# Transformer block pair with a 64-expert layer: shared expert's weights and a fourth set of expert places in dead arena rows

## The reference, cut to what matters

```python
def moe_ffn(h, w_router, b_router, w_e_gate, w_e_up, w_e_down, w_sh_gate, w_sh_up, w_sh_down):
    scores = jax.nn.sigmoid(h @ w_router)
    _, idx = lax.top_k(scores + b_router, TOP_K)            # 8 of 64 experts for each token
    ...
    yb = swiglu(h_pad[tok], w_e_gate[e], w_e_up[e], w_e_down[e]) * wt[:, None]
    ...
    return swiglu(h, w_sh_gate, w_sh_up, w_sh_down) + routed[:n]
```

## Time and profile before

| | |
|---|---|
| median of 3 runs | 1839.1 us (1836.88 to 1841.07) |
| the profiled execution's own time | 1846.18 us |
| its span (first to last instruction) | 1844.1 us |
| mean granted TensorE clock | 0.970 |
| PE, DVE, ACT, POOL busy | 91%, 45%, 30%, 2% |
| read from HBM | 416.07 MB, 227 GB/s over the span |
| SyncE's queue, share of 16 DMA engines | 58.8% |
| expert loop, first `pair_hidden` to the last one's start | 471.47 to 997.69 us |

### The profile page before, as it was taken

How to read it: one execution, slowest core, us unless ns; L and a number is a source line. 1 busy time by engine, 2 the same in 40 slices (tenths; PEclk the granted TensorE clock), 3 DMA queues, 4 the chain that set the end, 5 groups by cost and what they waited for, 6 DMA issues and landing times.

```text
span 1844.1 us, 22609 instructions
## 1 busy us (share of the span) xinstructions
PE 1675.3 (91%) x8972; PEld 1165.0 (63%) x8973; DVE 825.2 (45%) x1187; ACT 561.9 (30%) x795; POOL 41.4 (2%) x49
## 2 busy tenths in 40 slices
PE   2699999998899999899999799989999799989998
PEld 2674554546444444444444677779998677779997
DVE  1811982314322222222221676585444575675544
ACT  0001442002111111111111456644432456644441
POOL 2200000000000000000000000000000000000000
PEclk9999999998999999999999899989999899989999
DMA  9552488232899999899998443545554443535640
GB/s 261 180 209 97 168 306 309 102 98 89 327 374 392 375 395 387 350 388 387 382 381 339 145 165 121 200 137 182 169 176 163 148 147 137 190 130 183 206 160 23
DMA packets 148297, 418.62 MB, mean 227 GB/s; under 512 B 6960, under 2 KB 55104, under 8 KB 123168
## 3 DMA queue, kind: packets, MB, share of 16 engines
q1 hardware_dynamic: 143472, 399.12, 58.8%
q0 software_dynamic: 4720, 18.03, 3.2%
HBM read 416.07 MB, written 2.95 MB: 227 GB/s over the span
## 4 chain that ended last, share of the span: by engine, by line
PE 84%; DVE 7%; issue 5%; DMA 2%; ACT 1%; SPq 0%; DVEq 0%; ACTq 0%
PE bank L1414 14%; PE bank L1140 13%; PE bank L1241 12%; PE bank L847 9%; PE bank L1151 6%; PE bank L1394 6%; PE bank L1122 4%; PE bank L1161 3%; PE bank L816 3%; PE bank L1254 3%; PE bank L974 3%; DMA weight_ring<-in_w_ada 2%; PE bank L860 2%; DVE arena L1746 1%; DVE ring_low L2198 1%
## 5 line engine op out<-in xcount | busy, mean ns | idle before, releaser
L1140 PE MATMUL bank<-weight_ring,arena 128*64 128x512 f32 x1056 | 239.7, 607 | 40.2 <-issue 39.3
L2198 DVE TENSOR_TENSOR ring_low<-weight_ring,high_ring 128x2048 fp32r<-128x2048 f32 x94 | 211.5, 2288 | 62.2 <-ACT high_ring L1557 55.1
L1241 PE MATMUL bank<-high_ring,split 128*128 128x512 f32 x640 | 212.5, 406 | 0.0
L1140 PEld LDWEIGHTS bank<-weight_ring,arena 128*64 128x64 f32 x1056 | 87.5, 139 | 191.1 <-issue 191.1
L1414 PE MATMUL bank<-split,high_ring 128*128 128x256 f32 x1088 | 198.6, 286 | 3.1 <-issue 3.1
L1414 PE MATMUL bank<-split,ring_low 128*128 128x256 f32 x704 | 200.6, 285 | 0.0
L1557 ACT ACTIVATE high_ring<-weight_ring 128x2048 fp32r<-128x2048 f32 x94 | 175.2, 1903 | 17.7 <-PE bank L1241 8.5
L1414 PEld LDWEIGHTS bank<-split,high_ring 128*128 128x128 f32 x1088 | 170.9, 193 | 4.6 <-issue 3.9
L847 PE MATMUL bank<-weight_ring,arena 128*128 128x512 f32 (+1 forms) x416 | 163.2, 552 | 2.1 <-ACT arena L1447 1.3
L1241 PE MATMUL bank<-ring_low,split 128*128 128x512 f32 x384 | 154.0, 401 | 0.0
L1241 PEld LDWEIGHTS bank<-high_ring,split 128*128 128x128 f32 x640 | 124.0, 194 | 32.4 <-issue 3.4
(11 more groups left out here) (284 smaller groups left out, 2244.6 us busy)
## 6 DMA issues: line engine op xcount, KB each, us to landing
weight_ring<-in_w_e_gate SPq DMA_DIRECT2D x65, 1024.0 KB, 7.6
weight_ring<-in_w_e_up SPq DMA_DIRECT2D x65, 1024.0 KB, 9.7
weight_ring<-in_w_e_down SPq DMA_DIRECT2D x65, 1024.0 KB, 8.8
weight_ring<-in_w_in SPq DMA_DIRECT2D x62, 1024.0 KB, 7.3
weight_ring<-in_w_ada SPq DMA_DIRECT2D x24, 1024.0 KB, 11.5
weight_ring<-in_w_ffn_gate SPq DMA_DIRECT2D x22, 1024.0 KB, 5.5
weight_ring<-in_w_ffn_up SPq DMA_DIRECT2D x22, 1024.0 KB, 7.9
weight_ring<-in_w_ffn_down SPq DMA_DIRECT2D x22, 1024.0 KB, 6.4
```

The source lines that it names most:

```text
L1140: last = mm(hidden_bank[side * CAP:(side + 1) * CAP, :].rearrange("p (j n) -> p j n", n=FF), xgT[:, p // 2 % 2, kt, at:at + CAP], hidden_u ...
L1241: last = mm(bank(key)[:, :], left[:, a_, n, t * P:(t + 1) * P], wv[b_][:, j, :], start=(n == 0 and i == 0), stop=(n == kts * len(units_) - ...
L2198: V.tensor_tensor(lower(key), ring[:, units.place[key][0], :], upper(key), ALU.subtract)\
```

## The change

1. The shared expert's three matrices are no ring units any more. They go to the arena (`shared`, at 18432, 20480 and 12288), loaded by SyncE ahead of the last `wo` half, behind a wait for the last transpose of `u_` (`oaT`).
2. `GU_UNITS, DOWN_UNITS` are 4, 4. The fourth hidden unit lies in the arena at 10240 and 16384, the fourth down unit at 12288 (where the shared down was). The down units count from slot 8 downwards. Expert `e` uses unit `e % 4`.
3. The ring is moved on so that `upa` starts at slot 8: the last owners of slots 0 to 5 are then `upa`, `upb`, `upa`, `upa`, `upb`, `wo`, and of 6 to 8 `wo`.
4. The first loads stand in the order hidden 0, 1, 2, down 0, 1, 2, hidden 3, down 3. From pair 2 on the order is as it was.
5. `weighted` and `ys` move to other rows, and a sum of squares writes its product to `y` and not to `junk`. No instruction of TensorE, VectorE or ScalarE is added or taken away.

```diff
--- before.py
+++ after.py
@@ -50,7 +50,7 @@
 CHUNK = 512
 MASKED = -1e30
 SLOTS = 9
-GU_UNITS, DOWN_UNITS = 3, 3
+GU_UNITS, DOWN_UNITS = 4, 4
 SLOT = 2048
 ARENA = 30464
 DR = 6
@@ -232,6 +232,8 @@
             main.take(("sg", t, n))
     for g in range(4):
         main.take(("oaT", g))
+
+    units.at += (SLOTS - 1 - units.at) % SLOTS
     for n in range(2):
         chunk(("upa", n), ("upa", n, 1), "w_up_a", n * CHUNK)
         unit(("upb", n), ("upb", n, 1), "half", "w_up_b", n * CHUNK)
@@ -250,9 +252,6 @@
         main.take(("h2T", g))
     for t in range(TT):
         main.take(("rt", t))
-    unit(("shg",), ("shg", 1), "ff", "w_sh_gate", 0)
-    unit(("shu",), ("shg", 1), "ff", "w_sh_up", 0)
-    unit(("shd",), ("shared", 1), "down", "w_sh_down", 0)
     for f in range(2):
         main.take(("shg", f))
     for t in range(TT):
@@ -261,7 +260,7 @@
     last_jobs = {s: freed_by[units.owner[s]] for s in units.slots}
 
 
-    units.at += 2
+    units.at += (2 - units.at) % SLOTS
     for r in (main, long, hold, units):
         r.loop()
     for g in range(4):
@@ -499,7 +498,8 @@
         over = area(8400, TT, E)
         first, ranked = area(8528, E), area(8592, E)
         sil, hid, hidT = area(8704, 2, FF), area(9216, 2, FF), area(9728, 2, 2 * P)
-        weighted = area(10240, 2, TT, P)
+        weighted = area(29440, 2, TT, P)
+        shared = [area(at, SLOT) for at in (18432, 20480, 12288)]
         xgT = area(18432, 2, KT, QUAD * CAP)
         over_y = area(18432, 2, TT, CHUNK)
 
@@ -518,7 +518,7 @@
         fh32 = area(12288, 4, S)
 
         xs = split[:, 0:2 * KT * S].rearrange("p (w k t) -> p w k t", w=2, k=KT)
-        ys = split[:, 10752:10752 + 2 * D].rearrange("p (w d) -> p w d", w=2)
+        ys = split[:, 0:2 * D].rearrange("p (w d) -> p w d", w=2)
         h2s = routed[:, 0:2 * TT * D].rearrange("p (w t k f) -> p w t k f", w=2, t=TT, k=KT)
         h2k = h2.rearrange("p t (f k) -> p t k f", k=KT)
         onehot = routed[:, 4096:4096 + 2 * TT * QUAD * CAP].rearrange("p (b t s) -> p b t s", b=2, t=TT)
@@ -532,10 +532,12 @@
             return psum[3 + 2 * n + t]
 
         def hidden_unit(u):
-            return ring[:, 2 * u:2 * u + 2, :]
+
+            return ring[:, 2 * u:2 * u + 2, :] if u < GU_UNITS - 1 else area(10240, 2, 6144)[:, :, 0:SLOT]
 
         def down_unit(u):
-            return ring[:, 2 * GU_UNITS + u, :].rearrange("p (f n) -> p f n", n=D)
+            unit_ = ring[:, SLOTS - 1 - u, :] if u < DOWN_UNITS - 1 else area(12288, SLOT)
+            return unit_.rearrange("p (f n) -> p f n", n=D)
 
         def bank(key):
             return psum[banks[key][0]]
@@ -636,7 +638,7 @@
                         sp.wait_ge(sem("down_done"), (FT // 2 - 1) * (it + (0 if back else 1)) + job[1] + 1)
                         sp.sem_inc(sem("slots_freed"), 1)
                         continue
-                    if job[0] in ("ada_summed", "shared"):
+                    if job[0] == "ada_summed":
                         sp.wait_ge(sem(job[0]), job[1])
                         continue
                     at = (it - 1) if back else it
@@ -676,22 +678,28 @@
             sp.dma_start(cn, a["ctx"].rearrange("(t p) d -> p t d", p=P)).then_inc(sem("ctx_landed"), 16)
             sp.dma_start(const[:, :], a["consts"]).then_inc(sem("const_landed"), 16)
             for key in order:
+                if key == ("wo", 1, 1):
+
+                    wait_full(sp, ("oaT", 3))
+                    for j, (name, cols_) in enumerate((("w_sh_gate", FF), ("w_sh_up", FF), ("w_sh_down", D))):
+                        sp.dma_start(shared[j].rearrange("p (k n) -> p k n", n=cols_),
+                                     a[name].rearrange("(k p) n -> p k n", p=P)).then_inc(sem(f"shared_landed{j}"), 16)
                 if key[0] not in LAYER_KEYS:
                     load(key)
 
             def wait_slot(s):
-                job = last_jobs[s]
-                if job[0] == "shared":
-                    sp.wait_ge(sem("shared"), job[1])
-                else:
-                    b, n, per = banks[job]
-                    sp.wait_ge(bank_full[b], n + 1)
+                b, n, per = banks[last_jobs[s]]
+                sp.wait_ge(bank_full[b], n + 1)
 
             def load_hidden(e, i):
                 u = i % GU_UNITS
                 for j, name in enumerate(("w_e_gate", "w_e_up")):
-                    if i < GU_UNITS:
+                    if i < GU_UNITS - 1:
                         wait_slot(2 * u + j)
+                    elif i == GU_UNITS - 1:
+
+                        if j == 1:
+                            sp.wait_ge(sem("h2_ready"), TT)
                     elif j == 0:
                         sp.wait_ge(sem("hidden_full"), (i - GU_UNITS) // 2 + 1)
                     sp.dma_start(hidden_unit(u)[:, j, :].rearrange("p (k n) -> p k n", n=FF),
@@ -699,22 +707,31 @@
 
             def load_down(e, i):
                 u = i % DOWN_UNITS
-                if i < DOWN_UNITS:
-                    wait_slot(2 * GU_UNITS + u)
+                if i < DOWN_UNITS - 1:
+                    wait_slot(SLOTS - 1 - u)
+                elif i == DOWN_UNITS - 1:
+                    sp.wait_ge(sem("shared"), 1)
                 else:
                     sp.wait_ge(sem("down_full"), 2 * ((i - DOWN_UNITS) // 2 + 1))
                 sp.dma_start(down_unit(u), a["w_e_down"][e].rearrange("(p k) n -> p k n", p=P)).then_inc(sem(f"down_landed{u}"), 16)
 
             def expert_slot_free(s):
 
-                if s < 2 * GU_UNITS:
+                if s < 2 * (GU_UNITS - 1):
                     i = max(i for i in range(E + 1) if i % GU_UNITS == s // 2)
                     sp.wait_ge(sem("hidden_full"), i // 2 + 1)
                 else:
-                    i = max(i for i in range(E + 1) if i % DOWN_UNITS == s - 2 * GU_UNITS)
+                    i = max(i for i in range(E + 1) if i % DOWN_UNITS == SLOTS - 1 - s)
                     sp.wait_ge(sem("down_full"), 2 * (i // 2 + 1))
 
-            for p in range(PAIRS):
+
+            for e in range(3):
+                load_hidden(e, e)
+            for e in range(3):
+                load_down(e, e)
+            load_hidden(3, 3)
+            load_down(3, 3)
+            for p in range(2, PAIRS):
                 for side in range(2):
                     load_hidden(2 * p + side, 2 * p + side)
                 for side in range(2):
@@ -1072,19 +1089,15 @@
                               start=(kt == 0), stop=(kt == KT - 1))
                 full(last, ("rt", t))
 
-            def gate_up(key, right, gk, uk, f, f_in_unit, it=0):
-
-                wait_bank(pe, key, it)
-                for j, unit_key in enumerate((gk, uk)):
-                    wait_weights(pe, unit_key, it)
+            for f in range(2):
+                wait_bank(pe, ("shg", f))
+                for j in range(2):
+                    pe.wait_ge(sem(f"shared_landed{j}"), 16)
                     for kt in range(KT):
-                        last = mm(bank(key)[:, j * S:(j + 1) * S], w(unit_key, KT, FF)[:, kt, f_in_unit * P:(f_in_unit + 1) * P],
-                                  right[:, kt, :], start=(kt == 0), stop=(kt == KT - 1))
-                full(last, key)
-
-
-            for f in range(2):
-                gate_up(("shg", f), h2T, ("shg",), ("shu",), f, f)
+                        at = kt * FF + f * P
+                        last = mm(bank(("shg", f))[:, j * S:(j + 1) * S], shared[j][:, at:at + P], h2T[:, kt, :],
+                                  start=(kt == 0), stop=(kt == KT - 1))
+                full(last, ("shg", f))
 
             pe.wait_ge(sem("chosen"), TT)
             for t in range(TT):
@@ -1101,12 +1114,12 @@
 
             for f in range(2):
                 wait_out(pe, ("shg", f))
-            wait_weights(pe, ("shd",))
+            pe.wait_ge(sem("shared_landed2"), 16)
             for n in range(2):
                 for t in range(TT):
                     for f in range(2):
                         last = mm(y_bank(n, t)[:, :], ffs[:, f, t * P:(t + 1) * P],
-                                  w(("shd",), 2, D)[:, f, n * CHUNK:(n + 1) * CHUNK], start=(f == 0), stop=False)
+                                  shared[2][:, f * D + n * CHUNK:f * D + (n + 1) * CHUNK], start=(f == 0), stop=False)
             last.then_inc(sem("shared"), 1)
 
             def rows_in(i):
@@ -1970,7 +1983,7 @@
                     wait_out(dve, ("wo", n, t))
                     step(V.tensor_tensor(x[:, t, c], x[:, t, c], ga[:, t, c], ALU.add))
                 settle()
-                V.tensor_tensor_reduce(junk[:, 0:D], x[:, t, :], x[:, t, :], 1.0 / D, NORM_EPS,
+                V.tensor_tensor_reduce(y[:, t, :], x[:, t, :], x[:, t, :], 1.0 / D, NORM_EPS,
                                        ALU.mult, ALU.add, small[:, 24 + t:25 + t]).then_inc(sem("sums2"), 1)
                 step(V.tensor_tensor(h2[:, t, :], x[:, t, :], rows[:, 2, :], ALU.mult))
                 dve.wait_ge(sem("roots2"), t + 1)
```

## The result

The changed kernel takes 1792.95 us (median of 4 runs, 1789.12 to 1795.21) against 1837.99 us of the kernel before beside it. The ratio is 0.9753, 95% interval 0.9726 to 0.9781. The forecast was 1809.5 us with a range from 1796 to 1829: right in sign, too small in size, and the median lies 3 us outside the range.

A forecast was written before the change was run, and what follows sets the result against it. The prediction took transfers to bind the expert loop, TensorE close behind. More early loads and a faster pace together gained 29.6 us, other terms 0: 1809.5 us from a median of 1839.1, range 1796 to 1829.

The forecast's parts named there:

- What bounds the kernel before: Expert loop: bound by transfers at 381 GB/s, TensorE close behind; 16.44 us a pair against 15.08 clean.
- Part 1: Ahead of the expert loop: twelve expert loads issued early where eight were, saving 11.0 us.
- Rival D: Ahead of the loop: early loads are held up, only lookahead counts; within 0.2% of 1839.1 us; chance 0.05.
- Part 2: Expert loop: four places for three keep the queue from running dry; 395 GB/s, 183 units in 485.8 us.
- rival A: Expert loop: pace stays 381 GB/s, slow moments being the memory's; gain 11.7 us, 1827.4 us; chance 0.23.
- TensorE's floor: Expert loop: TensorE's own work takes 15.08 us a pair, capping the gain at 43.7 us.
- the waits add up to the same: Expert loop: TensorE's 39.3 us in 26 waits match the 1.36 us a pair above a clean one.
- Rival B: Expert loop: pace passes 405 GB/s, TensorE becomes the bound; gain 43.7 us, 1795.4 us; chance 0.18.
- rival C: Expert loop: the deep queue costs pace, 360 GB/s; 17.7 us slower, 1856.8 us; chance 0.03.
- Part 3: Before the loop: later `upa` and `upb` loads arrive in time; cost 0, bound 5.6 us.
- Part 4: Arena reads and everything after the loop: unchanged, 0; 5.5 us if the final norm's cover were gone.
- The clock: Expert loop: no wait of 3 us with a long hidden product after it, as once at granted clock 0.83.

The follow-up runs named there:

- x4: Changed kernel with hidden products over half of the contraction only, all transfers kept; 1778.3 us (one run).
- x2: Changed kernel with four places but only eight expert loads ahead of the loop, not twelve; 1798.5 us, 0.9775 of the kernel before.
- x1: Changed kernel with four places and twelve early loads, but later loads wait as with three places; 1834.98 us, 0.9972 of the kernel before.
- x6: Changed kernel with half of the hidden products and the waits of three places; 1792.48 us (one run).
- x9: Changed kernel with hidden loads waiting for their pair's down product, one batch of six loads a pair; 1797.66 us, 0.9771 of the kernel before.
- x8: Changed kernel where only the down loads wait as with three places; 1830.08 us, 0.9957 of the kernel before.
- x7: Changed kernel where only the hidden loads wait as with three places; 1834.92 us, 0.9973 of the kernel before.
- x12: Changed kernel without the shift of the ring and with first loads ordered by pairs; 1790.43 us, 0.9737 of the kernel before.
- x5: Changed kernel loading half of the bytes of every expert matrix, TensorE's work unchanged; 1788.87 us (one run).

## Why the prediction was wrong in size, point by point

**What bounds the kernel before.** Right in where: all of the gain lies between 471.7 and the last pair. Half right in what. The transfers held TensorE up, but they were not at their own end: they can do 421 GB/s, 14.9 us a pair (x4), TensorE 14.86, and a pair took 16.44. What cost 1.5 us a pair was the handing over of places between the two.

**Part 1, the stock, 11.0 us.** Too large, though it was the part of which I was "surest". Rival D, which took this part away, was priced even worse: "only the lookahead counts: within 0.2% of 1839.1", and in x2 the lookahead without the stock gave 2.3%. The count of units was right (twelve issued ahead of 478.80, for eight). But the saving was reckoned as if the queue went on without a break after 478.6. In x1, where the stock stands alone, the queue idles from 480 to 500 (share 0.55) and 5 us remain; in x2, where it is missing, 5.5 to 8 us are lost.

**Part 2, the pace with four places. This is the step that failed.** I took 395 GB/s, from the longest stretch with a share of 1.00, as "the pace of undisturbed stretches". It was not undisturbed. A busy DMA share only says that transfers are under way, not that they go at their best: the same stretch has 1.01 and 421 GB/s after. The loss of before had two parts, and I saw one. Per busy share the pace was 381 / 0.97 = 393 GB/s before and 373 / 0.95 = 393 in x1, and is 419 / 1.01 = 415 after: 3 to 5% were idle time of the queue, and another 5 to 6% were transfers that ran slower while the engines counted as busy. The trace has every packet of these loads, 128 of 8 KB for each. All 24960 of them together kept the 16 engines busy for 518.6 us before and 492.9 us after.

What ran slower is a small part of the packets. The median packet took 309 ns before and 312 after. But from 478.6 to 940 us 1067 of 21390 packets (5.0%) took over 400 ns before, 730 ns in the mean, and after it 64 of 23421 (0.3%). Of these long packets of before 88% start within 4 us after a load is issued, where 56% of all packets do. The third column of the table tells how full the queue still was when SyncE issued again after a pause of over 2 us: the packets issued and not begun, in loads of 128 packets, in the median.

| run | GB/s | loads left in the queue at a refill | packets over 400 ns |
|---|---|---|---|
| x4 | 421 | 5.7 | 0.1% |
| x2 | 421 | 4.6 | 0.1% |
| changed | 419 | 2.2 | 0.3% |
| x6 | 411 | 1.5 | 1.2% |
| x9 | 409 | 1.1 | 0.9% |
| x8 | 384 | 0.5 | 3.3% |
| x7 | 382 | 0.3 | 3.0% |
| before | 381 | 0.7 | 5.0% |
| x1 | 373 | 0.6 | 5.1% |

(x7, x8 and x9 refill once a pair, the others twice.) With less than one load left both losses are there in full: the queue stands idle for 4 to 6% of the time, and many of the packets behind a refill are long ones. x6 shows that both go nearly away when places come back early, with three places too. That TensorE's own work slows the transfers is excluded: it is busiest in the changed kernel, where they run at 419. Why packets behind a late refill take longer is not shown by these runs. The slow stretch of 360 GB/s at a share of 0.99, which I read as a hint of slow moments of the memory (rival A), fits the same reading: from 628 to 638 the changed kernel moves 424 GB/s, and in the nine slices of its page from 493 to 896 us 419 to 422.

**TensorE's floor, 15.08 us a pair, was also mis-sized, and it drew the range too narrow.** I took it from the pair 504.18 to 519.26 and called it clean. Its hidden product started after a wait of 2.87 us and took 7.09 us; one that follows without a wait takes 6.87, as the row at 519.26 already showed (6.88). The floor is 14.86 us. Over 32 pairs the 0.22 us are 7.0, so the largest gain was not 43.7 but 50.7 us, and the low end of the range should have been 1788, not 1796. The measured loop is 474.5 us long; 32 x 14.86 is 475.5, and the first pair is 0.93 shorter. This is also why "the waits add up to the same" was not quite so: the 1.36 us a pair over the clean one are 43.5 us, the waits 39.3. A wait costs more than its own length. TensorE's busy time itself fell by 10.8 us with the same 8972 matmuls (1675.3 before, 1664.5 after), since hidden products behind a wait took 7.09 us or, where the granted clock fell, up to 9.76; with the 39.3 us of waits that is 50.1 of the 51.5.

**Rival B was what happened**, at 0.18 against 0.50 for the forecast. Its condition, a pace above 405 GB/s, was met with 421. The Trainium skill (DMA: Bandwidth & Descriptors, Bandwidth) with 425 GB/s for a long transfer of a core alone agrees with the trace after, 419 over 461 us; I had weighed it too lightly because no long stretch before reached it. The limit of some 358 GB/s in the same page of the Trainium skill (Where 436 GB/s comes from), with which rival C went, does not hold for this core: the 419 GB/s over 461 us pass it.

**Part 3, later `upa` and `upb` loads, 0.** Right: the block of L864 starts at 356.07 behind the same work as before (355.96), and x12 with the old order of these loads is no faster.

**Part 4, arena places, shared weights, tail, 0.** Right: 847.0 us behind the last pair's start for 846.4, first layer product 34.8 us behind it for 34.4.

**The clock.** I expected no long hidden product after a wait any more. There are no waits for loads, and the granted clock is 1.00, the full 2.4 GHz, from 478.6 to 940 us, where the earlier trace rows had 0.83 in one stretch.

## What to carry to other kernels

When two engines hand buffers to each other and the trace shows one of them 97% busy, its rate in the busiest stretches is not yet its limit: measure that limit by taking work from the other engine (x4), and the other's floor by taking away bytes (x5), before putting a size on a change. Look also at how much the queue still holds when it is refilled: here the loss began at about one load left. A stock ahead of a loop and a deeper lookahead inside it are different things: here the stock alone gave 0.3%, the lookahead alone 2.3%. A floor for the bound engine must be read from a step that follows without a wait. The hidden product at 504.18 came behind one, and its first two matmuls took 614 and 643 ns where the others took 592.

## What the hardware showed that was not expected

With a queue that always held work, one core moved 419 to 422 GB/s from memory for 460 us, beside TensorE at 99.9% busy. With the same waits as the kernel before and TensorE's part made lighter it was 411, and with TensorE's full part 373, in 1 MiB transfers of one and the same form. The whole difference lies in idle time and in a few long packets of 730 ns behind late refills; the median packet of 8 KB took 309 to 312 ns in all of these runs. And on this one queue, in this order, the stock with a fourth place waited for in one of the two kinds of buffers only gave 0.3 to 0.4% (x7, x8), hardly more than the stock with none (x1, 0.3%); with both kinds it is 2.5%.
